# Expert weights of nine pairs loaded as whole 4 MB matrices instead of 2 MB halves, in a one-layer decoder step with a mixture of experts

## What is computed

```
logits = x2d @ router_w + router_b
top_vals, top_idx = lax.top_k(logits, TOP_K)          # 4 of 32
gates = jax.nn.softmax(top_vals, axis=-1)
...
gt  = jnp.minimum(xblk @ w_gate[e] + b_gate[e], SWIGLU_LIMIT)
up  = jnp.clip(xblk @ w_up[e] + b_up[e], -SWIGLU_LIMIT, SWIGLU_LIMIT)
hid = (up + 1.0) * (gt * jax.nn.sigmoid(SWIGLU_ALPHA * gt))
y   = hid @ w_down[e] + b_down[e]                     # summed with the gates
```

## Time and profile before

| | us |
|---|---|
| median of 3 runs | 1192.49 |
| lowest and highest | 1191.88, 1195.53 |
| the profiled execution's own time | 1193.42 |
| its span | 1191.7 |

### The profile page before, as it was taken

The page is one execution under the profiler, slowest core; times in us unless marked ns, Lnnn a source line. Parts: engine busy times, 40 slices in busy tenths (PEclk is TensorE's granted clock), DMA queues, the critical chain, the costliest instruction groups (busy, mean ns, idle before and its releaser), DMA issues.

```text
span 1191.7 us, 15436 instructions
## 1 busy us (share of the span) xinstructions
PE 1133.7 (95%) x5933; PEld 486.9 (41%) x5933; DVE 410.5 (34%) x779; ACT 215.7 (18%) x403; POOL 39.6 (3%) x118
## 2 busy tenths in 40 slices
PE   8999999999999999999999998999999999999997
PEld 6667865433333332333333333333333333332343
DVE  4756765833132221132223231313131313131325
ACT  3544232321101021011010101011010101010025
POOL 6002110000000000000000000000000000000000
PEclk9999999999999999999999999999999999999999
DMA  9921539889999999999999999999999999999941
GB/s 304 279 89 71 167 116 327 313 341 426 425 428 426 428 427 430 425 428 429 427 428 431 426 426 429 428 426 429 430 427 428 429 427 428 428 428 426 419 162 45
DMA packets 50603, 435.16 MB, mean 365 GB/s; under 512 B 6861, under 2 KB 14554, under 8 KB 24812
## 3 DMA queue, kind: packets, MB, share of 16 engines
q1 hardware_dynamic: 44425, 430.22, 87.4%
q10 hardware_dynamic: 6123, 4.18, 1.1%
HBM read 429.54 MB, written 4.11 MB: 364 GB/s over the span
## 4 chain that ended last, share of the span: by engine, by line
PE 69%; DMA 21%; DVE 5%; issue 2%; ACT 2%; POOL 0%; SPq 0%; DVEq 0%; ACTq 0%; POOLq 0%
PE ps L1798 40%; DMA ring<-in_w_gate 18%; PE ps L1318 7%; PE ps L1744 4%; PE ps L1635 3%; PE ps L1235 3%; DMA ring<-in_w_up 2%; PE ps L1524 2%; PE ps L1372 1%; PE ps L1439 1%; PE ps L1765 1%; DVE x_resid L2519 1%; PE ps L2012 1%; PE ps L1989 1%; PE ps L1870 1%
## 5 line engine op out<-in xcount | busy, mean ns | idle before, releaser
L1798 PE MATMUL ps<-ring,ht_region 128*64 128x512 f32 (+1 forms) x2152 | 452.8, 597 | 19.4 <-DMA ring<-in_w_gate 19.0
L1798 PEld LDWEIGHTS ps<-ring,ht_region 128*64 128x64 f32 (+1 forms) x2152 | 150.8, 134 | 306.0 <-issue 303.6
L1798 PE MATMUL ps<-ring,q_region 128*64 128x512 f32 (+1 forms) x1088 | 223.6, 594 | 0.3 <-ACT q_region L863 0.3
L1798 PEld LDWEIGHTS ps<-ring,q_region 128*64 128x64 f32 (+1 forms) x1088 | 71.7, 134 | 144.2 <-issue 143.3
L2519 DVE TENSOR_TENSOR x_resid<-ps,x_resid 128x512 f32<-128x512 f32 (+1 forms) x90 | 62.0, 688 | 148.0 <-PE ps L1744 143.8
L2569 DVE SCALAR_TENSOR_TENSOR q_region<-ps,small,u_region 128x1024 f32<-128x1024 f32 x15 | 19.3, 1284 | 222.9 <-ACT u_region L1107 222.9
L1318 PE MATMUL ps<-ht_region,ring 128*128 128x320 f32 x320 | 90.7, 441 | 1.3 <-ACT ht_region L878 0.7
L2561 DVE TENSOR_SCALAR q_region<-ps 128x1024 f32<-128x1024 f32 x15 | 18.4, 1224 | 165.4 <-PE ps L1798 165.3
L1318 PEld LDWEIGHTS ps<-ht_region,ring 128*128 128x128 f32 x320 | 60.8, 193 | 27.6 <-issue 3.9
L1085 ACT ACTIVATE q_region<-q_region 128x1024 f32<-128x1024 f32 x16 | 16.9, 1057 | 292.0 <-DVE q_region L2543 292.0
L1107 ACT ACTIVATE u_region<-ps,small 128x1024 bf16<-128x1024 f32 x15 | 16.7, 1113 | 226.9 <-PE ps L1798 226.9
(11 more groups left out here) (510 smaller groups left out, 908.2 us busy)
## 6 DMA issues: line engine op xcount, KB each, us to landing
ring<-in_w_gate SPq DMA_DIRECT2D x62, 2048.0 KB, 25.0
ring<-in_w_up SPq DMA_DIRECT2D x62, 2048.0 KB, 22.2
ring<-in_w_down SPq DMA_DIRECT2D x57, 2048.0 KB, 27.0
ring<-in_w_down SPq DMA_DIRECT2D x13, 1024.0 KB, 24.7
ring<-in_w_in SPq DMA_DIRECT2D x4, 2048.0 KB, 17.7
ring<-in_w_out SPq DMA_DIRECT2D x2, 2048.0 KB, 9.4
ring<-in_w_up SPq DMA_DIRECT2D x4, 1024.0 KB, 25.0
ring<-in_w_ple_gate SPq DMA_DIRECT2D x2, 2048.0 KB, 22.3
```

Source lines behind the costliest of these rows:

```text
L1798: ins = mm(PS[s0_:s0_ + width, b0 + hf, :], lhs[:, k, s0_:s0_ + width], rows[:, kk, hf * 512:(hf + 1) * 512], start=False, stop=(k == KT - 1),
```

## The change

In pairs 3 to 7 and 9 to 12 SP issues a whole matrix as one transfer of 4 MB. `load_matrix` writes slots c and c + 2 (first and second half of one expert's matrix, as before), with two runs of 16 KB per partition. Before it, SP waits for the release of the later of the two slots, `used(cc + 2 + a_ - RING)`, and the order in a product becomes all of a, then all of b. The landing steps only `chunk_in` of the first half; that of the second half is stepped by a no-op on SP right behind the issue. So TensorE's program stays as it is, and its wait for the first halves now stands for the whole matrices. Pairs 1 and 2 are written out ahead of the loop instead of in it, and pairs 8, 13, 14 and 15 keep their transfers.

```diff
+        def load_matrix(eng, c, e, s):
+
+            cc = c % CPP
+            w = chunk_src["gud"[cc // CPM]][bass.ds(e, 1)]
+            eng.dma_start(ring[:, c % RING:c % RING + 3:2, :],
+                          w.rearrange("a (m p k) f -> p (a m) (k f)", p=P, k=RPP)).then_inc(s, 16)
...
-            def turn_loads(lo, hi):
-
-                with sp.Fori(lo, hi - 1) as i:
-                    pair_loads(i, 1)
-                    pair_loads(i + 1, 0)
-                if hi < TURNS:
-                    pair_loads(hi - 1, 1)
-                    return
+            def pair_matrices(turn, half):
+
+                es = experts_of(turn * 2 + half)
+                for c in range(0, CPP, CPM):
+                    cc = half * CPP + c
+                    for a_ in range(2):
+                        sp.wait_ge(chunk_used, turn * (2 * TURN) + used(cc + 2 + a_ - RING))
+                        load_matrix(sp, cc + a_, es[a_], chunk_in[cc + a_])
+                        sp.nop().then_inc(chunk_in[cc + 2 + a_], 16)
...
+            def first_turn_loads():
+
+                pair_loads(0, 1)
+                pair_loads(1, 0)
...
-            turn_loads(0, MID)
+            first_turn_loads()
+            with sp.Fori(1, MID - 1) as i:
+                pair_matrices(i, 1)
+                pair_matrices(i + 1, 0)
+            pair_matrices(MID - 1, 1)
...
-            turn_loads(MID, TURNS)
+            with sp.Fori(MID, TURNS - 2) as i:
+                pair_matrices(i, 1)
+                pair_matrices(i + 1, 0)
+            pair_loads(TURNS - 2, 1)
+            pair_loads(TURNS - 1, 0)
+            last_pair_loads()
```

More of the change, by code:

```diff
@@ L657, in pair_loads, with last_pair_loads @@
                     load_chunk(sp, cc, es, chunk_in[cc])
-            def turn_loads(lo, hi):
-                with sp.Fori(lo, hi - 1) as i:
-                    pair_loads(i, 1)
-                    pair_loads(i + 1, 0)
-                if hi < TURNS:
-                    pair_loads(hi - 1, 1)
-                    return
+            def pair_matrices(turn, half):
[6 more added lines that the diff above has]
+                        sp.nop().then_inc(chunk_in[cc + 2 + a_], 16)
+            def last_pair_loads():
+                hi = TURNS
                 es = experts_of(2 * hi - 1)
```

## The result

| | before | after |
|---|---|---|
| median, us | 1193.45 | 1213.07 |
| lowest and highest | 1191.88, 1195.53 | 1212.75, 1215.88 |
| profiled execution, span | 1193.42, 1191.7 | 1213.01, 1211.3 |

The median before is here of four runs, one more than in the first table. The changed kernel takes 1.0168 times as long (95% interval 1.0150 to 1.0185). The direction was right, the size was not.

The account below looks back on a forecast made before the run. The transfer queue bounds the kernel: its empty time is lost, TensorE's mostly not. Losses 8.8 + 2.1 + 0.5 = 11.4 us take the profiled 1193.42 to 1204.8, the median 1192.49 to 1203.9; range 1197.0 to 1212.5.

Parts of the forecast that it names:

- No gain per transfer: 54 fewer transfers in nine pairs: taken as 0 us gained, with 5.4 us kept as an end.
- The hole at pair 4's down loads: Pair 4's down loads wait for the gate product's end, 472.71, with the queue empty since 467.06: 8.8 us lost.
- Pair 5's up loads: Issued at 513.89, 1.2 us before the gate weights land: 2.1 us lost.
- the prediction's rule: A transfer must be issued 3.2 us before the last one lands; each us less is lost.
- Pair 4's up loads: Issued 3.05 us before the gate weights land, just enough: 0.15 us lost, left out of the sum.
- The last is short by 0.1 us, in five pairs 0.5 us: Repeating cycle after pair 5: the load issued 3.1 us ahead loses 0.1 us, in five pairs 0.5 us.
- an allowance: Lower clock after a wait delays down's end 1.2 us and the next up load: once or twice, up to 2.5 us.
- More lead needed: Rival: a 4 MB transfer needs more lead than a 2 MB one, e.g. 4.6 us: 19.7 us lost, 1212.2; chance 0.12.
- The gain per transfer: Rival: each of 54 saved transfers gains 0.10 us, leaving 6.0 us lost, 1198.5; chance 0.08.
- the other side: Rival: larger transfers in nine pairs run so much better that the kernel is not slower, from 0.21 us each; chance 0.14.
- The tail of 95 us: Span after the last wait for gate weights follows TensorE: it stays, starting about 11 us later.
- A hole in every pair: Sign that the prediction is wrong: the queue running empty in every pair.

Follow-up runs that it names:

- late issue alone: Kernel before, its nine pairs still in 2 MB loads, but a product's first chunk is issued only when the whole old product is done; TensorE's waits unchanged: 1198.42 us, 1.0034.
- late wait alone: Kernel before with its loads unchanged, but TensorE waits for all four chunks in pairs 3 to 7 and 9 to 12: 1202.2 us, 1.0063.

## Why the prediction was right in direction and short in size

- **What bounds the kernel: right.** Every loss of the queue came out at the end; TensorE's extra work before cost nothing.
- **No gain per transfer: right.** 9.79 us for 4 MB, and 1212.45 with twice as many transfers.
- **The hole at pair 4's down loads: right in place and cause, in size partly by luck.** 8.8 was forecast and 9.0 measured, at 467 to 475 as said. But pair 4's gate product ran 15.65 us, so the down loads went out at 474.50 instead of 472.71, and the up loads ahead of them lost 2.4 us, so the queue ran dry at 469.05 instead of 467.06. The two errors cancel. The Trainium skill (DMA: Bandwidth & Descriptors, "Rules for kernel authors") says to issue early and wait late; the change does the opposite, and the trace agrees with the rule: late issue alone cost 4.1 us, late wait alone 7.5. Behind the empty queue the load needed 3.6 us beyond its bytes (9.0 - 5.4); the 2.0 us that the prediction took from that page of the Trainium skill ("Anatomy of one DMA") is given for the gpsimd path, and these loads go out on SP.
- **Pair 5's up loads: 2.1 forecast, 1.9 measured, by luck.** The forecast had a lead of 1.2, and it was 2.9, for which the prediction's rule gives 0.3.
- **Pair 4's up loads, "0.15 lost, left out": wrong, 2.4.** Their forecast lead was 3.05, the measured 2.5.
- **"The last is short by 0.1 us, in five pairs 0.5 us": wrong, 5.5.** This is the step that failed, with the one above it: a lead of 3.1 us was taken as just enough and priced at next to nothing. Together the two lost 7.9 us, against 0.65 worked out. With the up loads alone in halves 1213.07 became 1206.8, and with 2.1 us more TensorE work 1221.46, so the place is shown. Another 2.6 us went in smaller pieces that the sum didn't have, and the earlier start of the stream takes 1.2 off.

Two things made it so. The first is the leads. Forecast were 3.1 us for each; measured, 2.6, 3.15, 1.6, 3.2 and 2.2. Pairs 10 and 12 are short because the gate product ahead, of pairs 9 and 11, ran 15.77 and 15.65 us instead of 13.95. The prediction had that case as an allowance, once or twice, and left it out of the sum; it came in six of the nine pairs. Pair 6 is short because pair 5's gap from up to down was 8.41, not 8.04. By the prediction's own rule (3.2 less the lead) these leads give 0.6 + 0.05 + 1.6 + 0 + 1.0 = 3.3 us of the 5.5.

The second is the rule, and it is the larger part: for the up loads of all seven pairs 4 to 7 and 10 to 12 it gives 4.3 us with the measured leads, and they lost 9.8. It came from one row, of a load whose lead was 1.1. In the traces of all seventeen kernels there are 146 weight loads issued between 270 and 1080 us with leads under 5 us. Grouped by lead, with what was lost at the load:

| lead, us | loads | mean lost | least and most | 3.2 less the mean lead |
|---|---|---|---|---|
| under -2 | 10 | 8.0 | 5.4, 11.8 | 7.7 |
| -2 to 0 | 5 | 4.1 | 3.6, 4.7 | 4.2 |
| 0 to 2 | 10 | 2.0 | 1.4, 3.3 | 1.9 |
| 2 to 2.6 | 18 | 2.0 | 0.6, 3.0 | 0.9 |
| 2.6 to 3.2 | 26 | 1.1 | 0, 2.4 | 0.3 |
| 3.2 to 3.8 | 25 | 0.5 | 0, 1.6 | 0 |
| 3.8 to 4.4 | 33 | 0.2 | 0, 1.3 | 0 |
| 4.4 to 5 | 19 | 0.0 | 0, 0.3 | 0 |

With an empty queue 3.2 is a fair price. At the edge it is not: the need (the lead and what was lost) scatters from 2.7 to 5.3 us, a load that needs less gives nothing back, one that needs more loses. So leads of 3.0 to 3.2 cost 0.8 us on average (9 loads, 0 to 2.0), not 0.1. What sets the need of a single load is open. The forecast's lead stood just there, five times.

- **The rivals.** More lead needed had 1212.2 for 0.12, nearest to the measured time; but the need does not grow with the size: 2 MB loads for each matrix gave 1212.45, and in the table's group of 2 to 2.6 us the 2 MB loads lost 2.2 on average (3 loads), those of 4 MB 2.0 (15). The range left the worst of this case out and was too narrow by that. The gain per transfer and the other side did not show.
- **The tail of 95 us and TensorE's waits from pair 3 on: right.** At gate's start in pairs 6, 7 and 10 to 12 it waits 1.2 to 2.8 us, where some 3 were forecast. "A hole in every pair" was named as a sign of being wrong, and small ones did open in nearly every one.

## What to carry to other kernels

A coarser release costs lead in every cycle: write down the lead of each load over one steady cycle, and take off what may delay the consumer there (a product at the lower clock, a gap that varies), before saying that it suffices. A lead just equal to the need is not free; price it with the scatter, not with one row. And a stall that TensorE causes needn't go away when the load where it shows is split: in the one case tried here it went to the next whole release. Look at the releases behind it too, or remove the lateness.

## What the runs showed of the hardware

- Transfers of 4 MB with a full queue land 9.79 us apart, those of 2 MB 4.895: the rate is the same.
- A load issued into an empty queue landed, counted from its issue, 2.7 to 4.2 us later than its bytes take (15 loads of all runs, 3.3 on average); with leads up to 5 us, the loads that lost time needed 2.7 to 5.3 us.
- A full queue now and then loses about 1.5 us at one load: twice in the kernel after, with leads of 19 and 23 us, and twice in before, with 15 and 25. Why is open.
- Six of the nine gate products of the kernel after took 15.6 to 15.8 us, with a granted clock of 0.74 to 0.77 over their first 7 us. Five of them stood behind waits for weights of 2.2 to 7.3 us, pair 4's behind one of 2.6 us on ScalarE. The other three took 13.95 us, at 1.00, behind waits of 1.2 to 2.5 us, and so did pair 4's in the kernel before, behind 2.8 us. With matmuls ahead of eight of the nine, all nine took 13.95 us.
